# Routing of a mixture of experts: scores with tokens on the partitions from the router product on, choice of the experts by a vector chain over single experts

## The reference, cut to what matters

```python
def moe(h, router_w, router_b, w_gate, w_up, w_down):
    t = h.reshape(-1, D_MODEL)
    scores = jax.nn.sigmoid((t @ router_w).astype(jnp.float32))
    sel = scores + router_b.astype(jnp.float32)
    grouped = sel.reshape(-1, N_EXPERT_GROUPS, EXPERTS_PER_GROUP)
    group_score = lax.top_k(grouped, TOP_K)[0].sum(-1)
    g_idx = jnp.argmax(group_score, axis=-1)
    ...
    _, local = lax.top_k(in_group, TOP_K)
    expert_idx = g_idx[:, None] * EXPERTS_PER_GROUP + local
    wts = jnp.take_along_axis(scores, expert_idx, axis=1)
    wts = wts / jnp.sum(wts, axis=-1, keepdims=True)
    combine = jnp.sum(jax.nn.one_hot(expert_idx, N_EXPERTS) * wts[..., None], axis=1)
```

## Time and profile before

| | |
|---|---|
| time, median of 3 runs | 2490.15 us (2487.81 to 2498.6) |
| the profiled execution | 2490.15 us, span 2488.4 us |
| instructions in the span | 36177 |
| first routing, from the last scaled tile of h to the next stage | 1358.32 to 1375.36 us of the span |
| second routing, the same | 2110.28 to 2122.22 us of the span |

### The profile page before, as it was taken

The page is one execution under the profiler, slowest core; times in us unless marked ns, Lnnn a source line. Parts: engine busy times, 40 slices in busy tenths (PEclk is TensorE's granted clock), DMA queues, the critical chain, the costliest instruction groups (busy, mean ns, idle before and its releaser), DMA issues. The chain is left out here.

```text
span 2488.4 us, 36177 instructions
## 1 busy us (share of the span) xinstructions
PE 2173.9 (87%) x12264; PEld 1776.2 (71%) x12264; DVE 1702.1 (68%) x2820; ACT 1360.2 (55%) x2127; POOL 280.9 (11%) x355
## 2 busy tenths in 40 slices
PE   4999899889998999858888799995889886799993
PEld 4899876589995666647665678783777774677782
DVE  5884626278554699876554699994477753699993
ACT  2663425166453355655433578883476641588882
POOL 0000000000000365555000001001000000010100
PEclk8999999999998999969899899996999888899996
DMA  6455431545543666400021699995221112699991
GB/s 219 161 187 170 145 106 43 199 155 197 170 140 137 249 239 237 153 0 2 26 75 54 247 390 391 387 390 189 83 77 60 58 53 68 248 397 394 393 358 68
DMA packets 127254, 454.96 MB, mean 183 GB/s; under 512 B 13824, under 2 KB 17792, under 8 KB 126976
## 3 DMA queue, kind: packets, MB, share of 16 engines
q1 hardware_dynamic: 116160, 413.14, 45.7%
q0 software_dynamic: 10944, 39.85, 4.2%
HBM read 431.97 MB, written 20.97 MB: 182 GB/s over the span
## 5 line engine op out<-in xcount | busy, mean ns | idle before, releaser
L2707 DVE TENSOR_TENSOR moe_w_lo<-ring,moe_w_hi 128x1024 fp32r<-128x1024 f32 x384 | 462.8, 1222 | 61.5 <-ACT moe_w_hi L2645 56.5
L2645 ACT CAST moe_w_hi<-ring 128x1024 fp32r<-128x1024 f32 x384 | 399.0, 1048 | 131.6 <-PE ps L236 120.7
L373 DVE TENSOR_TENSOR ffn_w_lo<-ring,ffn_w_hi 128x1024 fp32r<-128x1024 f32 x132 | 161.0, 1222 | 101.2 <-ACT ffn_w_hi L325 101.0
L234 PE MATMUL ps<-moe_w_hi,moe_own 128*128 128x512 f32 x512 | 214.6, 419 | 12.2 <-DVE moe_own L2714 11.1
L235 PE MATMUL ps<-moe_w_lo,moe_own 128*128 128x512 f32 x512 | 205.6, 401 | 0.0
L236 PE MATMUL ps<-moe_w_hi,moe_own 128*128 128x512 f32 x512 | 205.4, 401 | 0.0
L325 ACT CAST ffn_w_hi<-ring 128x1024 fp32r<-128x1024 f32 x132 | 137.4, 1044 | 107.5 <-PE ps L236 107.4
L234 PE MATMUL ps<-ffn_h_hi,ffn_w_hi 128*128 128x256 f32 x608 | 173.7, 286 | 11.2 <-DVE ffn_w_lo L373 11.2
L235 PE MATMUL ps<-ffn_h_lo,ffn_w_hi 128*128 128x256 f32 x608 | 172.4, 284 | 0.0
L236 PE MATMUL ps<-ffn_h_hi,ffn_w_lo 128*128 128x256 f32 x608 | 172.3, 283 | 0.0
L2557 POOL DMA_INDIRECT moe_got<-token_rows,moe_idx x32 | 44.6, 1394 | 877.2 <-DVE moe_idx L2702 877.2
(11 more groups left out here) (540 smaller groups left out, 5611.7 us busy)
## 6 DMA issues: line engine op xcount, KB each, us to landing
ring<-in_weights SPq DMA_DIRECT2D x766, 512.0 KB, 5.3
expert_rows<-moe_y POOLq DMA_DIRECT2D x32, 512.0 KB, 7.1
token_rows<-moe_token_rows SPq DMA_DIRECT2D x6, 512.0 KB, 3.7
sq<-in_cmp_w SPq DMA_DIRECT2D x1, 2048.0 KB, 7.6
both<-in_x SPq DMA_DIRECT2D x1, 1024.0 KB, 5.9
both<-in_context SPq DMA_DIRECT2D x1, 1024.0 KB, 8.2
out<-both SPq DMA_DIRECT2D x1, 1024.0 KB, 4.8
cols<-in_cols SPq DMA_DIRECT2D x1, 720.5 KB, 9.2
```

Of the source, the lines that this page charges most:

```text
L234: pe.matmul(out, w_hi, x_hi, start=start, stop=False)
L373: dve.tensor_tensor(w_lo[:, u % WB], k.ring[:, (first + u) % RING], w_hi[:, u % WB], ALU.subtract).then_inc(w_split, 1)
L2645: act.copy(w_hi[:, j % WB].rearrange("p h f -> p (h f)"), k.slot(act, first + GU + j, e).rearrange("p a f -> p (a f)")).then_inc(w_rounded, 1)
L2707: dve.tensor_tensor(w_lo[:, j % WB].rearrange("p h f -> p (h f)"), k.ring[:, (first + GU + j) % RING].rearrange("p a f -> p (a f)"), w_hi[ ...
```

## The change

In `moe_route` the sides of the router product are exchanged: for each tile of 128 tokens, eight products with a tile of h as the stationary side and the 16 router columns as the moving side. The product begins when all of h is ready. The scores then have tokens on the partitions; ScalarE takes the sigmoid of all of them in one instruction into `score`, and the turning of the scores with its two hand-overs is gone, as is the later copy of the scores.

The choice of the experts no longer uses `ranks`. The sum of each group's best two is made from the four experts' columns by maxima and minima; the group is the one equal to the largest, the first such if there are several; the rank in the group comes from the six pairs of experts, four instructions each. A drain stands behind each of these instructions.

The place sums of each token tile are formed on their own (1 + 2 + 3 + 4 products for four tiles), the total of each expert goes into the same bank of PSUM, and one signal, `placed`, stands behind them all.

```diff
@@ -2363,15 +2363,12 @@
 
         score = sb("score", [P, tt_n, EGROUPS, EPG])
         sel = sb("sel", [P, tt_n, EGROUPS, EPG])
-        beaten = sb("beaten", [P, tt_n, EGROUPS, EPG, EPG])
-        g_beaten = sb("g_beaten", [P, tt_n, EGROUPS, EGROUPS])
-        g_score, g_rank = sb("g_score", [P, tt_n, EGROUPS]), sb("g_rank", [P, tt_n, EGROUPS])
-        across = sb("across", [EXPERTS, n])
+        w3 = sb("w3", [P, 8, tt_n * EGROUPS])
         rank = sb("rank", [P, tt_n, EGROUPS, EPG])
         top = sb("top", [P, 4, tt_n])
-        with stage_semaphores(nc, f"{name}_route", *NORM_SEMS, "made", "ready", "routed", "scored", "score_turned", "picked",
-                              "placed", "counted", "turned", "kept", "rows_stored") as sems, nc.Block(name=f"{name}_route", no_gpsimd_drain=True) as block:
-            norm, (made, ready, routed, scored, score_turned, picked, placed, counted, turned, kept, rows_stored) = sems[:4], sems[4:]
+        with stage_semaphores(nc, f"{name}_route", *NORM_SEMS, "made", "ready", "routed", "scored", "picked", "placed",
+                              "turned", "kept", "rows_stored") as sems, nc.Block(name=f"{name}_route", no_gpsimd_drain=True) as block:
+            norm, (made, ready, routed, scored, picked, placed, turned, kept, rows_stored) = sems[:4], sems[4:]
             UNITS, BANKS = 2 * tt_n, 4
 
             @block.sync
@@ -2384,15 +2381,12 @@
             @block.tensor
             def _(pe):
                 norm_tensor(k, pe, norm, n)
-                for t in range(KD):
-                    pe.wait_ge(ready, (t + 1) * len(segs))
-                    mm = pe.matmul(k.ps[0:EXPERTS, 6, 0:n], router_w[:, t, :], k.h[:, t, 0:n], start=(t == 0), stop=(t == KD - 1))
+                pe.wait_ge(ready, KD * len(segs))
+                for tt in range(tt_n):
+                    for t in range(KD):
+                        mm = pe.matmul(k.ps[:, 6, tt * EXPERTS:(tt + 1) * EXPERTS], k.h[:, t, tt * P:(tt + 1) * P],
+                                       router_w[:, t, :], start=(t == 0), stop=(t == KD - 1))
                 mm.then_inc(routed, 1)
-                pe.wait_ge(scored, 1)
-                for tt in range(tt_n):
-                    mm = pe.transpose(k.ps[:, 5, tt * EXPERTS:(tt + 1) * EXPERTS], across[:, tt * P:(tt + 1) * P],
-                                      k.ident[0:EXPERTS, 0:EXPERTS])
-                mm.then_inc(score_turned, 1)
                 for u in range(UNITS):
                     if u >= BANKS:
                         pe.wait_ge(kept, u - BANKS + 1)
@@ -2402,22 +2396,22 @@
                     mm.then_inc(turned, 1)
                 pe.wait_ge(picked, 1)
 
-                picks = chosen[:, :, :].rearrange("p t e -> p (t e)")
-                mm = pe.matmul(k.ps[:, NORM_BANK, 0:tt_n * EXPERTS], k.upto[:, :], picks, start=True, stop=False, skip_group_check=True)
-                for s in range(1, tt_n):
-                    mm = pe.matmul(k.ps[:, NORM_BANK, s * EXPERTS:tt_n * EXPERTS], k.ones[:, :], picks[:, 0:(tt_n - s) * EXPERTS],
-                                   start=False, stop=(s == tt_n - 1), skip_group_check=True)
+                for tt in range(tt_n):
+                    for s in range(tt + 1):
+                        pe.matmul(k.ps[:, NORM_BANK, tt * EXPERTS:(tt + 1) * EXPERTS], k.upto[:, :] if s == tt else k.ones[:, :],
+                                  chosen[:, s, :], start=(s == 0), stop=(s == tt))
+                for s in range(tt_n):
+                    mm = pe.matmul(k.ps[:, NORM_BANK, tt_n * EXPERTS:(tt_n + 1) * EXPERTS], k.ones[:, :], chosen[:, s, :],
+                                   start=(s == 0), stop=(s == tt_n - 1))
                 mm.then_inc(placed, 1)
-                for s in range(tt_n):
-                    mm = pe.matmul(k.ps[:, 6, 0:EXPERTS], k.ones[:, :], chosen[:, s, :], start=(s == 0), stop=(s == tt_n - 1))
-                mm.then_inc(counted, 1)
 
             @block.scalar
             def _(act):
                 norm_scalar(k, act, norm, xin, n)
                 mod_norm_shift(k, act, segs, shift, made, ready)
                 act.wait_ge(routed, 1)
-                act.activation(across[:, :], k.ps[0:EXPERTS, 6, 0:n], ACT.Sigmoid).then_inc(scored, 1)
+                act.activation(score[:, :, :, :].rearrange("p t g e -> p (t g e)"), k.ps[:, 6, 0:tt_n * EXPERTS], ACT.Sigmoid
+                               ).then_inc(scored, 1)
                 for u in range(UNITS):
                     act.wait_ge(turned, u + 1)
                     act.copy(rows[:, u // 2, u % 2 * 512:(u % 2 + 1) * 512], k.ps[:, u % BANKS, :]).then_inc(kept, 1)
@@ -2425,49 +2419,56 @@
             @block.vector
             def _(dve):
                 mod_norm_vector(k, dve, norm, x, segs, gain, n, made)
+                dve.wait_ge(scored, 1)
                 G = tt_n * EGROUPS
                 s4 = score[:, :, :, :].rearrange("p t g e -> p (t g) e")
                 v4 = sel[:, :, :, :].rearrange("p t g e -> p (t g) e")
                 r4 = rank[:, :, :, :].rearrange("p t g e -> p (t g) e")
-                b4 = beaten[:, :, :, :, :].rearrange("p t g i j -> p (t g) i j")
+                wk = [w3[:, i, :] for i in range(8)]
 
                 def tt_(o, a, b, op):
                     dve.tensor_tensor(o, a, b, op)
                     dve.drain()
 
-                def ranks(to, of, wins, many):
-
-                    for i in range(many):
-                        own = of[:, :, i:i + 1]
-                        if i:
-                            dve.tensor_tensor(wins[:, :, i, 0:i], of[:, :, 0:i], own.broadcast_to([P, of.shape[1], i]), ALU.is_ge)
-                        if i + 1 < many:
-                            dve.tensor_tensor(wins[:, :, i, i + 1:], of[:, :, i + 1:], own.broadcast_to([P, of.shape[1], many - i - 1]),
-                                              ALU.is_gt)
-                    dve.drain()
-                    dve.tensor_reduce(to, wins, AX.X, ALU.add)
-                    dve.drain()
-
-                dve.memset(beaten[:, :, :, :, :], 0.0)
-                dve.memset(g_beaten[:, :, :, :], 0.0)
-                dve.wait_ge(score_turned, 1)
-                turned_scores = k.ps[:, 5, 0:tt_n * EXPERTS].rearrange("p (t e) -> p t e", t=tt_n)
-                tt_(sel[:, :, :, :].rearrange("p t g e -> p t (g e)"), turned_scores,
+                tt_(sel[:, :, :, :].rearrange("p t g e -> p t (g e)"), score[:, :, :, :].rearrange("p t g e -> p t (g e)"),
                     router_b.unsqueeze(1).broadcast_to([P, tt_n, EXPERTS]), ALU.add)
-                ranks(r4, v4, b4, EPG)
-                dve.tensor_scalar(r4, r4, TOPK - 0.5, None, ALU.is_lt)
+                e = [v4[:, :, i] for i in range(EPG)]
+
+                tt_(wk[0], e[0], e[1], ALU.max)
+                tt_(wk[1], e[0], e[1], ALU.min)
+                tt_(wk[2], e[2], e[3], ALU.max)
+                tt_(wk[3], e[2], e[3], ALU.min)
+                tt_(wk[4], wk[0], wk[2], ALU.max)
+                tt_(wk[5], wk[0], wk[2], ALU.min)
+                tt_(wk[6], wk[1], wk[3], ALU.max)
+                tt_(wk[5], wk[5], wk[6], ALU.max)
+                tt_(wk[4], wk[4], wk[5], ALU.add)
+
+                gs = wk[4].rearrange("p (t g) -> p t g", g=EGROUPS)
+                isg = wk[5].rearrange("p (t g) -> p t g", g=EGROUPS)
+                dve.tensor_reduce(top[:, 0, :], gs, AX.X, ALU.max)
                 dve.drain()
-                tt_(b4[:, :, 0, :], r4, v4, ALU.mult)
-                dve.tensor_reduce(g_score[:, :, :].rearrange("p t g -> p (t g)"), b4[:, :, 0, :], AX.X, ALU.add)
+                tt_(isg, gs, top[:, 0, :].unsqueeze(2).broadcast_to([P, tt_n, EGROUPS]), ALU.is_equal)
+                dve.memset(top[:, 1, :], 1.0)
                 dve.drain()
-                ranks(g_rank[:, :, :], g_score[:, :, :], g_beaten[:, :, :, :], EGROUPS)
-                dve.tensor_scalar(g_rank[:, :, :], g_rank[:, :, :], 0.5, None, ALU.is_lt)
+                for g in range(EGROUPS):
+                    tt_(isg[:, :, g], isg[:, :, g], top[:, 1, :], ALU.mult)
+                    tt_(top[:, 1, :], top[:, 1, :], isg[:, :, g], ALU.subtract)
+
+                dve.memset(rank[:, :, :, :], 0.0)
+                dve.drain()
+                for i in range(EPG):
+                    for j in range(i + 1, EPG):
+                        tt_(wk[0], e[j], e[i], ALU.is_gt)
+                        tt_(r4[:, :, i], r4[:, :, i], wk[0], ALU.add)
+                        dve.tensor_scalar(wk[1], wk[0], -1.0, 1.0, ALU.mult, ALU.add)
+                        dve.drain()
+                        tt_(r4[:, :, j], r4[:, :, j], wk[1], ALU.add)
+                dve.tensor_scalar(rank[:, :, :, :], rank[:, :, :, :], TOPK - 0.5, None, ALU.is_lt)
                 dve.drain()
                 c4 = chosen[:, :, :].rearrange("p t (g e) -> p (t g) e", g=EGROUPS)
-                tt_(c4, r4, g_rank[:, :, :].rearrange("p t g -> p (t g)").unsqueeze(2).broadcast_to([P, G, EPG]), ALU.mult)
```

(6 more changed lines are left out.)

## The result

The changed kernel takes 2523.45 us (median of 4 runs, 2518.55 to 2526.71) against 2491.02 for the kernel before (4 runs); the ratio is 1.0125, with a 95% interval of 1.0094 to 1.0154. Slower by 32.4 us; 29.7 were forecast, and 2523.45 lies in the range of 2506 to 2526. The profiled execution took 2520.72 us, its span is 2518.9: 30.5 us longer than before.

What follows compares the result with a forecast made beforehand. The routings were taken to add one for one, since the weight stream cannot run ahead: +17.7 us in the first and +12.0 in the second, 29.7 on 2490.15, gave 2520 us; range 2506 to 2526.

Steps and rivals of the forecast that it cites:

- What bounds it: Whole kernel: expert stages bound by the weight stream, which cannot run ahead, so longer routings lengthen the kernel one for one.
- The router product: TensorE in both routings: waits for all of h, then 64 and 32 instructions at 0.214 us, ending at 1372.9 and 2118.0.
- Rival 1: TensorE in the routings: clock rises in the product and is high in the sums; 2513, or 2508 if high throughout; 20%.
- Sigmoid and turn: ScalarE behind the router product: sigmoid 0.21 and 0.19 us; the transposes of the scores, 0.42 us, and a hand-over go.
- The vector chain: Vector engine, bias to chosen experts: 48 instructions, drained ones at 0.245 us, 11.7 us in each routing.
- rival 3: Small instructions in the routings dearer, 0.30 us for each of the 94 vector ones: +5.2 us, 2525; 8%.
- Rival 2: Vector engine in the routings: drained instructions cost nearer the undrained 0.09 us, 7.3 us less per chain; 2507; 6%.
- Rank sums and tail: End of the routings: 28 and 10 sum instructions at 0.214 us, 6.2 and 2.4 us; rest of the tail stays.
- The row stores do not decide: End of the first routing: stores would allow the next stage at 1387.6, before the vector engine's path at 1393.1.
- Rival 4: Both routings: cost goes with width, so not slower; 2483, within 0.5% of before; 6% together with anything unseen.

Runs made afterwards that it cites:

- the idle products: Changed kernel with 12 and 7 unread 512-column products on TensorE while it waits for h, ahead of the router product: 2520.89 us, ratio 1.0122.
- the kernel with the early product: Changed kernel with the router product begun at the first shifted tile, each token tile's sums in a bank of their own: 2523.7 us, ratio 1.0116.
- the chain alone: Kernel before with only the choice of the experts by the new vector instructions, product and rank sums as before: 2510.8 us, ratio 1.0057.
- the old sums: Changed kernel with the rank sums of the kernel before: 2522.96 us, ratio 1.0118.
- the warmed sums: Changed kernel with unread 512-column products ahead of the router product and 9 and 10 more ahead of the rank sums: 2520.63 us, ratio 1.0111.

## Why the prediction was right

- **What bounds it.** Right: the two routings make 30.15 of the 30.5 us of the span. The expert stages are 0.40 and 1.08 us shorter (334.13 against 334.53, 330.64 against 331.72), within what they differ by between kernels. That all the rest adds up to +0.35 us is in part luck, since the mixer's stretch alone differs by up to 12.7 us between executions.
- **The router product.** Right in mechanism and size: 13.84 and 7.01 us against 13.86 and 7.0. The row that carried it was that of the same form, 128x128 stationary and 16 columns, back to back at 0.50. That the price is the clock's is shown by the idle products: 0.11 us at the upper level. The 0.13 us that the forecast had for that level was too high: it is 1.04 us over 8 instructions and holds the longer last one, where 0.214 is taken from start to start, so 64 of them at 1.00 would take some 7.3 us and not 8.3.
- **Rival 1, the clock rises in the product.** It did not: in no kernel here did the clock rise in a router product of this form. Where such a product began at the upper level (the second routing of the kernel with the early product, both routings of the kernels with idle products ahead), the clock fell in the middle of it.
- **Sigmoid and turn.** 0.23 and 0.20 us against 0.21 and 0.19.
- **The vector chain.** The first was mis-sized: 12.51 us against 11.7. A drained instruction of 16 elements stood 0.25 or 0.26 us from the next (0.245 taken), and 0.43 us of idle time is the stall without a releaser, which the chain alone has too; that is a part of the way to rival 3. In the second, 11.60 us against 11.7. Rival 2 is refuted by these distances; that an instruction costs less where no drain follows is shown by the kernel with fewer drains (five comparisons in 0.57 us).
- **Rank sums and tail.** 6.15 and 2.31 us, as forecast, at the lower clock as forecast; shown with the old sums (-3.08 and -0.85) and with the warmed sums. TensorE idles 7.5 us before the first of them, not some 4: the transposes of h took 5.51 us and not double their 3.71, because the clock rose during them. That was off the path.
- **The row stores do not decide.** Right: they landed before the vector engine was done; from the last copy to the next stage the 6.26 us taken as fixed are not (4.19 and 4.55 in other kernels). In the changed kernel that does not count, but the length of the kernel before holds these 6.26 us; with 4.55 its first routing would be 1.7 us shorter and the step to the changed one as much longer. That the same 1375.36 stood in forecast and comparison hides this.
- **Rival 4, cost by width.** Refuted by both prices.

The median lies 3.4 us above the forecast. 0.9 us of it is the kernel before, whose median is 2491.02 and not 2490.15 with its fourth run, and 0.8 the span of the profile (30.5 against 29.7); the rest lies inside the spread of the runs. The mechanism is checked by the routings, not by this median: in other kernels here the median missed the routings by up to 10 us, so that it came so close is in part luck.

## What to carry to other kernels

Turning a product round so that the small side moves can multiply its instructions, and in these traces each of 16 columns costs as much as one of 128 (0.111 us at the upper clock, as in the 32 transposes of 3.71 us; 0.214 at the lower). Count the instructions, and look up the granted clock where a row of the same form stands: the 16-column products here did not bring the clock up in 13.84 us and did not keep it. A chain of short vector instructions costs by its drains (12.51 us with 48, 7.32 with 22); group what is independent between two of them. Price an edit together with the others: the rank sums were free alone and cost 3.9 us behind a chain that took their cover and their clock.

## What was not expected of the hardware

- With TensorE busy without a gap, the granted clock fell from 1.00 to 0.50 during a series of 16-column matmuls, 0.95 us after 10.5 us of 512-column ones at 1.00. In the second routing of the kernel with the early product it fell too.
- In the changed kernel the clock rose during the 128-column transposes right behind the product in which it had stayed at 0.50.
- An untouched stretch of some 395 us differs by up to 12.7 us between profiled executions, at mean granted clocks of 0.86 to 0.89.
- A median of a few runs can hide 9.7 us that a stage's trace shows plainly: two kernels with the same routings to 0.03 us have medians of 2512.54 and 2523.7 us.
